# Differential attention on one Trainium2 core: the difference of the two probability maps is made by two matrix products with diagonals of the inverse sums, in place of scaling on VectorE and transposes

## The chip, the cores and the metric

One core of one Trainium2 chip runs the whole program. The time is the device time of one execution in microseconds, and the median of several executions is compared. TensorE (PE in the profile) does the matrix products, VectorE (DVE), ScalarE (ACT) and GpSimd (POOL) the elementwise work; the queues of SyncE (SP) and of ScalarE issue the DMAs.

## The reference

The program is a chain of three transformer blocks over 512 positions of width 1024. Only the attention of the second block is touched. It has 4 heads, each with two maps m = 0, 1 of 64 query and key channels and a common value of 128 channels:

```
logits = einsum('bqhmd,bkhmd->bhmqk', q_blk, k) * scale + bias   # bias by distance, per head
logits = where(causal, logits, -inf)
p = softmax(logits, axis=-1)
attn = p[:, :, 0] - lam_full * p[:, :, 1]
o = einsum('bhqk,bkhe->bqhe', attn, v)
o = rms_norm(o, subln_g, eps=1e-5) * (1.0 - lambda_init)
```

`lam_full` is one number, worked out once from four small vectors. Beside the attention stands a short gated convolution over the other 512 channels, and both go together through one output projection.

## The kernel before, in words

The program is a list of stages. Each stage has a method per engine (`pe`, `act`, `dve`), which writes that engine's instructions in a fixed order by hand; semaphores tie the engines together, and nothing is scheduled by a planner. SyncE streams the weights of the large projections in panels of 1 MB, two buffers deep; it issues nothing that belongs to the attention itself.

The stage is `DiffAttention` (from line 1274 on). Its work is cut into 16 units, head h = 0..3 by query block b = 0..3; unit (h, b) has 128 queries and `nk` = 128(b+1) keys, so one to four key blocks of 128, 40 key blocks over the 16 units. All data are float32. Per unit:

- TensorE makes the logits of each map (lines 1418 and 1419): a product of q and k over 64 rows of the array, and onto it a product of a flipped identity with the bias table, `nk` columns each.
- VectorE takes the maximum of each row (1337) and negates it (1339); ScalarE takes the exponential with that bias and sums each row (1307), which leaves the unnormalised maps in `d_p[:, 0]` and `d_p[:, 1]`, three units deep.
- VectorE takes the reciprocals of both sums (1344), scales map 0 by its own (1346), multiplies the other reciprocal by minus lambda (1347), and adds map 1 times that onto map 0 (1349). Then `probs_ready` is signalled.
- TensorE transposes the difference, one 128x128 block after another, into PSUM bank 5 or 6 (1425).
- VectorE copies the transposed row of blocks to SBUF (1353).
- TensorE multiplies the values with it (1434), accumulated over the key blocks in bank 4 or 7.

The engines run skewed. In its step n TensorE makes the logits of unit n, the transposes of unit n-2 and the products with the values of unit n-3. VectorE in its step n takes the maxima of unit n, the normalisation of unit n-1 and the copy of unit n-2. At the end of a head ScalarE takes the result out and squares it (1295, 1296), TensorE makes its mean squares with products of two columns (1399), VectorE keeps them in `R` (1392, at the top of its steps 8 and 12 for heads 0 and 1), and only then may TensorE transpose the values of the head after the next into the same bank (1411), ahead of that head's first logits.

After the last unit follow the convolution on VectorE and ScalarE (1355 to 1370), 16 diagonals of the inverse roots (1377), their spreading by products with ones (1446), the normalisation (1382) and the split of the result into two parts (1384, 1387). Then the output projection begins (301 to 303). The two products of lines 1425 and 1434 read blocks of 128 columns; `d_w`, which the change adds, lies in the first 768 words of `d_diag`, whose 2048 words are written only after the last unit.

Of the kernel before, what the change touches and what calls it, by code (L numbers as in the profile page):

```python
# [23 lines left out]
ALU = mybir.AluOpType  # L24
# [357 lines left out]
class Stage:  # L382
# [13 lines left out]
    def dve(self, K, P):  # L396
        pass
# [876 lines left out]
class DiffAttention(Stage):  # L1274
# [52 lines left out]
    def dve(self, K, P):  # L1327
        e = P.e
        for n in range(self.N + 2):
            if n >= 8 and n % 4 == 0:  # L1330
                self.keep_mean(K, P, n // 4 - 2)
            if n < self.N:
                h, b = self.UNITS[n]
                nk, st = 128 * (b + 1), K.d_st[:, n % 3]
                for m in range(2):
                    P.e.wait_ge(P.sem("logits_done"), P.due("logits_done"))
                    e.reduce_max(st[:, m, 0:1], K.PS[:, 2 * (n % 2) + m, 0:nk], AX.X).then_inc(P.sem("dve_order"), P.adds("dve_order"))
                    P.e.wait_ge(P.sem("dve_order"), P.due("dve_order", 0))
                    e.tensor_scalar(st[:, m, 1:2], st[:, m, 0:1], -1.0, None, ALU.mult).then_inc(P.sem("max_negated"), P.adds("max_negated"))
            if 1 <= n <= self.N:  # L1340
                nk, st = 128 * (self.UNITS[n - 1][1] + 1), K.d_st[:, (n - 1) % 3]
                p0, p1 = (K.d_p[:, m, (n - 1) % 3, 0:nk] for m in range(2))
                P.e.wait_ge(P.sem("exp_done"), P.due("exp_done", 2))
                e.reciprocal(st[:, :, 3:4], st[:, :, 2:3]).then_inc(P.sem("dve_order"), P.adds("dve_order"))
                P.e.wait_ge(P.sem("dve_order"), P.due("dve_order", 0))
                e.tensor_scalar(p0, p0, st[:, 0, 3:4], None, ALU.mult)
                e.tensor_scalar(st[:, 1, 3:4], st[:, 1, 3:4], K.lamt[:, 5:6], None, ALU.mult).then_inc(P.sem("dve_order"), P.adds("dve_order"))
                P.e.wait_ge(P.sem("dve_order"), P.due("dve_order", 0))
                e.scalar_tensor_tensor(p0, p1, st[:, 1, 3:4], p0, ALU.mult, ALU.add).then_inc(P.sem("probs_ready"), P.adds("probs_ready"))
            if n >= 2:  # L1350
                nk = 128 * (self.UNITS[n - 2][1] + 1)
                P.e.wait_ge(P.sem("probs_transposed"), P.due("probs_transposed"))
                e.tensor_copy(K.d_pT[:, n % 2, 0:nk], K.PS[:, 5 + n % 2, 0:nk]).then_inc(P.sem("probsT_ready"), P.adds("probsT_ready"))

        e.tensor_tensor(K.in2[:, 16:20, :], K.in2[:, 16:20, :], K.in2[:, 20:24, :], ALU.mult).then_inc(P.sem("conv_z"), P.adds("conv_z"))
        self.keep_mean(K, P, 3)
        r = K.R[:, 0:16]
        P.e.wait_ge(P.sem("mean_kept"), P.due("mean_kept", 0))

        e.tensor_scalar(r, r, 1e-5, None, ALU.add).then_inc(P.sem("dve_order"), P.adds("dve_order"))  # L1360
        P.e.wait_ge(P.sem("dve_order"), P.due("dve_order", 0))
        e.reciprocal(r, r).then_inc(P.sem("o_inverse"), P.adds("o_inverse"))
        for i in range(4):
            z, y = K.in2[:, 16 + i, :], K.in2[:, 20 + i, :]
            P.e.wait_ge(P.sem("conv_seeded"), P.due("conv_seeded"))
            e.scalar_tensor_tensor(y[:, 1:S], z[:, 0:S - 1], K.p["conv2_w1"][:, i:i + 1], y[:, 1:S], ALU.mult, ALU.add).then_inc(P.sem("dve_order"), P.adds("dve_order"))
            P.e.wait_ge(P.sem("dve_order"), P.due("dve_order", 0))
            e.scalar_tensor_tensor(y[:, 2:S], z[:, 0:S - 2], K.p["conv2_w0"][:, i:i + 1], y[:, 2:S], ALU.mult, ALU.add).then_inc(P.sem("dve_order"), P.adds("dve_order"))
        P.e.wait_ge(P.sem("dve_order"), P.due("dve_order", 0))
        e.tensor_tensor(K.in2[:, 16:20, :], K.in2[:, 20:24, :], K.in2[:, 12:16, :], ALU.mult).then_inc(P.sem("conv_gated"), P.adds("conv_gated"))  # L1370
        P.e.wait_ge(P.sem("o_root"), P.due("o_root"))

        e.tensor_scalar(r, r, 0.8, None, ALU.mult).then_inc(P.sem("dve_order"), P.adds("dve_order"))
        P.e.wait_ge(P.sem("dve_order"), P.due("dve_order", 0))
        for h in range(4):
            for j in range(4):
                last = e.tensor_scalar(K.d_diag[:, h, 128 * j:128 * j + 128], K.ident[:, :], K.R[:, 4 * h + j:4 * h + j + 1], None, ALU.mult)
            last.then_inc(P.sem("o_diagonals"), P.adds("o_diagonals"))
        for h in range(4):
            P.e.wait_ge(P.sem("o_spread"), P.due("o_spread"))  # L1380
            o = K.in2[:, h, :]
            e.scalar_tensor_tensor(o, o, K.p["subln_g"][:, 0:1], K.PS[:, h, :], ALU.mult, ALU.mult).then_inc(P.sem("o_normed"), P.adds("o_normed"))
        P.e.wait_ge(P.sem("conv_hi"), P.due("conv_hi"))
        e.tensor_tensor(K.XL[:, 4:8, 0:S], K.in2[:, 16:20, :], K.XH[:, 4:8, 0:S].bitcast(F32), ALU.subtract)
        for h in range(4):
            P.e.wait_ge(P.sem("o_hi"), P.due("o_hi"))
            e.tensor_tensor(K.XL[:, h, 0:S], K.in2[:, h, :], K.XH[:, h, 0:S].bitcast(F32), ALU.subtract)
        P.count("att_out_done", 4)
# [5 lines left out]
    def pe(self, K, P):  # L1394
# [7 lines left out]
        for n in range(self.N + 3):  # L1402
            if n < self.N:
                h, b = self.UNITS[n]
                nk = 128 * (b + 1)
                if b == 0:
# [3 lines left out]
                    for j in range(4):  # L1410
                        last = P.e.transpose(K.PS[:, (4, 7)[h % 2], 128 * j:128 * j + 128], K.in2[:, h + 8, 128 * j:128 * j + 128], K.ident[:, :])
# [8 lines left out]
            if 2 <= n < self.N + 2:  # L1420
                m = n - 2
                P.e.wait_ge(P.sem("probs_ready"), P.due("probs_ready"))
                for kb in range(self.UNITS[m][1] + 1):
                    c = slice(128 * kb, 128 * kb + 128)
                    last = P.e.transpose(K.PS[:, 5 + m % 2, c], K.d_p[:, 0, m % 3, c], K.ident[:, :])
                last.then_inc(P.sem("probs_transposed"), P.adds("probs_transposed"))
            if n >= 3:
                h, b = self.UNITS[n - 3]
# [3 lines left out]
                for kb in range(b + 1):  # L1432
                    c = slice(128 * kb, 128 * kb + 128)
                    last = P.e.matmul(K.PS[:, (4, 7)[h % 2], 128 * b:128 * b + 128], K.d_vT[:, h % 2, c],
                                      K.d_pT[:, (n - 3) % 2, c], start=(kb == 0), stop=(kb == b))
# [6 lines left out]
        for h in range(4):  # L1442
            P.e.wait_ge(P.sem("o_diagonals"), P.due("o_diagonals"))
            for j in range(4):
                c = slice(128 * j, 128 * j + 128)
                last = P.e.matmul(K.PS[:, h, c], K.ones_row[:, 0:128], K.d_diag[:, h, c], start=True, stop=True)
# [1068 lines left out]
def program(nc, args, out):  # L2515
    n_panels = args["weights"].shape[0]
    with ExitStack() as ctx:
        K, M = Places(), Mem(nc)
# [34 lines left out]
        def v(name, shape, words, base=None, dt=F32):  # L2553

            assert words + int(np.prod(shape[1:])) <= (room if base is None else 24 * S), (name, room)
            return nc.alloc_sbuf_tensor_at(name, shape, dt, offset=(scr if base is None else base) + 4 * words)
# [26 lines left out]
        K.d_q, K.d_k = (nc.alloc_sbuf_tensor_at(n, [128, 2, 2, S], F32, offset=xa + 4 * 2048 * j) for j, n in enumerate(("d_q", "d_k")))  # L2583
        K.d_p = nc.alloc_sbuf_tensor_at("d_p", [128, 2, 3, S], F32, offset=xb)
        K.d_vT, K.d_pT, K.d_diag = v("d_vT", [128, 2, S], 0), v("d_pT", [128, 2, S], 1024), v("d_diag", [128, 4, S], 2048)
        K.bias, K.d_st, K.lam = v("bias", [128, 4, 512], 5120), v("d_st", [128, 3, 2, 4], 4096), v("lam", [128, 256], 7184)
        K.lamt, K.bias_t, K.onehot = v("lamt", [128, 8], 7440), v("bias_t", [33, 4], 7448), v("onehot", [33, BIAS_W], 7456)
        K.d_sq = v("d_sq", [128, S], 9128)
# [260 lines left out]
```

## Time and profile before

| what | value |
| --- | --- |
| median of 3 runs | 4536.89 us (4536.65 to 4537.7) |
| the profiled execution, its own time | 4535.49 us |
| its span | 4533.7 us |
| mean granted TensorE clock | 0.908 |
| TensorE busy | 3973.9 us, 88% |
| VectorE busy | 2244.2 us, 50% |
| ScalarE busy | 1281.1 us, 28% |
| DiffAttention, first logits to start of the output projection | 1707.8 to 1820.3 us |

The span is the time from the first to the last instruction of the profiled execution, 1.8 us less than its own time; that time is 1.4 us under the median. The clock is given as a share of full speed: 0.50 is 1.2 GHz and 1.00 is 2.4 GHz. A float32 product appears as two MATMULs with a LDWEIGHTS each; a transpose as one of each. Start times of the timeline are in us from the start of the span, and where several instructions are merged the duration is that of all of them, with the last one's latency.

### The profile page before, as it was taken

Reading aid. Unit: us, or ns where it says so; the run is one execution under the profiler, and the core shown is the slowest. Engines: PE = TensorE matmul, PEld = TensorE weight load, DVE = VectorE, ACT = ScalarE, POOL = GpSimd, SP = SyncE. Lnnn points to the kernel's source line nnn. Section 1 sums busy time; section 2 is a strip of 40 time slices with the busy share of each in tenths; the row PEclk is TensorE's granted clock in tenths of the full one; section 3 lists DMA queues with packets and bytes.
Section 4 is the critical chain, followed back from the end, with each engine's and each line's share of the span. In section 5 each row is a group of like instructions: output and inputs, shape, how many; then the busy total and the mean of one; then the engine's idle time right before and its main releaser. Section 6 shows DMA issues by size and latency. Waiting matters only on the chain. (4 is left out here: it accounts for less than half of the span.)

```text
span 4533.7 us, 54286 instructions
## 1 busy us (share of the span) xinstructions
PE 3973.9 (88%) x20865; PEld 3148.3 (69%) x20865; DVE 2244.2 (50%) x3393; ACT 1281.1 (28%) x1779; POOL 0.2 (0%) x4
## 2 busy tenths in 40 slices
PE   7789999978999898799989899782799956998998
PEld 6567887767788774688766688571577734676886
DVE  3475565344646535543443634437566645425344
ACT  2353333221433313222231322223211122223222
POOL 0000000000000000000000000000000000000000
PEclk9999999976999997899997999895899967899998
DMA  3102222210222220122220222220000000022221
GB/s 124 56 0 77 99 93 93 93 37 0 89 97 93 84 95 10 56 93 93 93 80 28 74 93 93 71 73 0 5 0 0 0 13 25 10 83 75 101 95 65
DMA packets 43352, 278.45 MB, mean 61 GB/s; under 512 B 5921, under 2 KB 6817, under 8 KB 10599
## 3 DMA queue, kind: packets, MB, share of 16 engines
q1 hardware_dynamic: 36576, 266.35, 16.7%
q10 hardware_dynamic: 6662, 10.53, 0.7%
q8 instruction: 78, 1.28, 0.1%
q14 instruction: 36, 0.29, 0.0%
HBM read 274.76 MB, written 2.11 MB: 61 GB/s over the span
## 5 line engine op out<-in xcount | busy, mean ns | idle before, releaser
L213 PE MATMUL PS<-XH,WH 128*128 128x512 f32 (+1 forms) x2704 | 1042.7, 386 | 27.3 <-DVEq L95 23.5
L214 PE MATMUL PS<-XL,WH 128*128 128x512 f32 (+1 forms) x2704 | 1044.1, 386 | 0.0
L215 PE MATMUL PS<-XH,WL 128*128 128x512 f32 (+1 forms) x2704 | 1038.7, 384 | 0.0
L146 DVE TENSOR_TENSOR WL<-W,WH 128x2048 fp32r<-128x2048 f32 x254 | 582.1, 2292 | 885.4 <-ACT WH L136 879.9
L136 ACT ACTIVATE WH<-W 128x2048 fp32r<-128x2048 f32 x254 | 485.5, 1912 | 1225.7 <-PE PS L303 681.1
L213 PEld LDWEIGHTS PS<-XH,WH 128*128 128x128 f32 x2704 | 510.6, 189 | 145.2 <-issue 20.2
L214 PEld LDWEIGHTS PS<-XL,WH 128*128 128x128 f32 x2704 | 510.0, 189 | 108.2 <-issue 2.2
L215 PEld LDWEIGHTS PS<-XH,WL 128*128 128x128 f32 x2704 | 511.1, 189 | 103.9
L301 PE MATMUL PS<-HH,WH 128*128 128x512 f32 (+1 forms) x1024 | 402.2, 393 | 10.5 <-DVEq L95 9.3
L484 DVE TENSOR_TENSOR PS<-PS,R 128x512 f32<-128x512 f32 x248 | 171.3, 697 | 467.3 <-PE PS L215 466.8
L302 PE MATMUL PS<-HL,WH 128*128 128x512 f32 (+1 forms) x1024 | 400.3, 391 | 0.0
L303 PE MATMUL PS<-HH,WL 128*128 128x512 f32 (+1 forms) x1024 | 400.0, 391 | 0.0
L301 PEld LDWEIGHTS PS<-HH,WH 128*128 128x128 f32 x1024 | 193.2, 189 | 56.0 <-DVEq L95 10.2
L303 PEld LDWEIGHTS PS<-HH,WL 128*128 128x128 f32 x1024 | 193.2, 189 | 40.5
L302 PEld LDWEIGHTS PS<-HL,WH 128*128 128x128 f32 x1024 | 193.4, 189 | 39.6
L301 PE MATMUL PS<-XH,WH 128*128 128x512 f32 x320 | 130.0, 406 | 26.6 <-DVEq L95 26.6
L736 ACT ACTIVATE CV<-PS,params 128x512 f32<-128x512 f32 x88 | 67.9, 778 | 245.0 <-DVE PS L484 245.0
L302 PE MATMUL PS<-XL,WH 128*128 128x512 f32 x320 | 128.4, 401 | 0.0
L303 PE MATMUL PS<-XH,WL 128*128 128x512 f32 x320 | 128.2, 401 | 0.0
L187 PE MATMUL PS<-XH,WH 128*128 128x512 f32 x144 | 62.2, 432 | 74.4 <-DVE XL L448 74.4
L301 PEld LDWEIGHTS PS<-XH,WH 128*128 128x128 f32 x320 | 62.0, 194 | 42.0 <-DVEq L95 28.1
L187 PEld LDWEIGHTS PS<-XH,WH 128*128 128x128 f32 x144 | 30.0, 208 | 83.9 <-issue 77.0
(446 smaller groups left out, 5220.3 us busy)
## 6 DMA issues: line engine op xcount, KB each, us to landing
W<-in_weights SPq DMA_DIRECT2D x254, 1024.0 KB, 4.8
X<-in_x ACTq DMA_DIRECT2D x1, 2048.0 KB
out<-X ACTq DMA_DIRECT2D x1, 2048.0 KB, 7.1
consts<-in_consts ACTq DMA_DIRECT2D x1, 1026.0 KB
bias<-bias_spread ACTq DMA_DIRECT2D x4, 256.0 KB
w_gd<-in_w_gd ACTq DMA_DIRECT2D x1, 640.0 KB
rope<-in_c_rope ACTq DMA_DIRECT2D x1, 528.0 KB
ws<-in_ws ACTq DMA_DIRECT2D x1, 512.0 KB
```

The lines of the kernel that those rows point to most:

```text
L136: P.e.activation(K.WH[:, s, :], K.W[:, s, :], ACT.Copy).then_inc(P.sem("hi_ready"), P.adds("hi_ready"))
L146: P.e.tensor_tensor(K.WL[:, s, :], K.W[:, s, :], K.WH[:, s, :].bitcast(F32), ALU.subtract).then_inc(P.sem("weights_split"), P.adds("weight ...
L187: P.e.matmul(out, wh[:, k, c], xh[:, k, 0:S], start=(k == 0), stop=False)
L213: P.e.matmul(out, wh[:, k, c], xh[:, k, r], start=(k == 0), stop=False)
L214: P.e.matmul(out, wh[:, k, c], xl[:, k, r], start=False, stop=False)
L215: last = P.e.matmul(out, wl[:, k, c], xh[:, k, r], start=False, stop=(k == KT - 1))
L301: P.e.matmul(out, K.WH[:, s, c], h, start=(first and kk == 0), stop=False)
L302: P.e.matmul(out, K.WH[:, s, c], l, start=False, stop=False)
L303: last = P.e.matmul(out, K.WL[:, s, c], h, start=False, stop=(last_panel and kk == 1))
L484: P.e.tensor_tensor(ps, ps, K.RB[:, :], ALU.mult).then_inc(P.sem("tile_scaled"), P.adds("tile_scaled"))
L736: P.e.activation(K.CV[:, s, t, :], ps[t], ACT.Identity, bias=b[:, c], scale=w[2][:, c]).then_inc(P.sem("conv_seeded"), P.adds("conv_seeded"))
```

## The change

Per unit VectorE no longer touches the maps. From the two reciprocals it makes two diagonal matrices of 128x128: the identity times the inverse sums of map 0, and the identity times the inverse sums of map 1 times minus lambda. TensorE then makes each transposed block of the difference as two float32 products that accumulate in PSUM: block of map 0 against the first diagonal, block of map 1 against the second. The wait on `dve_order` between the old instructions 1347 and 1349 goes with them. Nothing else is moved; no DMA and no ScalarE instruction is touched.

```diff
             if 1 <= n <= self.N:
                 nk, st = 128 * (self.UNITS[n - 1][1] + 1), K.d_st[:, (n - 1) % 3]
-                p0, p1 = (K.d_p[:, m, (n - 1) % 3, 0:nk] for m in range(2))
                 P.e.wait_ge(P.sem("exp_done"), P.due("exp_done", 2))
                 e.reciprocal(st[:, :, 3:4], st[:, :, 2:3]).then_inc(P.sem("dve_order"), P.adds("dve_order"))
                 P.e.wait_ge(P.sem("dve_order"), P.due("dve_order", 0))
-                e.tensor_scalar(p0, p0, st[:, 0, 3:4], None, ALU.mult)
-                e.tensor_scalar(st[:, 1, 3:4], st[:, 1, 3:4], K.lamt[:, 5:6], None, ALU.mult).then_inc(P.sem("dve_order"), P.adds("dve_order"))
-                P.e.wait_ge(P.sem("dve_order"), P.due("dve_order", 0))
-                e.scalar_tensor_tensor(p0, p1, st[:, 1, 3:4], p0, ALU.mult, ALU.add).then_inc(P.sem("probs_ready"), P.adds("probs_ready"))
+                w = K.d_w[:, (n - 1) % 3]
+                e.tensor_scalar(w[:, 0, :], K.ident[:, :], st[:, 0, 3:4], None, ALU.mult)
+                e.tensor_scalar(w[:, 1, :], K.ident[:, :], st[:, 1, 3:4], K.lamt[:, 5:6], ALU.mult, ALU.mult).then_inc(P.sem("probs_ready"), P.adds("probs_ready"))
...
                 for kb in range(self.UNITS[m][1] + 1):
                     c = slice(128 * kb, 128 * kb + 128)
-                    last = P.e.transpose(K.PS[:, 5 + m % 2, c], K.d_p[:, 0, m % 3, c], K.ident[:, :])
+                    P.e.matmul(K.PS[:, 5 + m % 2, c], K.d_p[:, 0, m % 3, c], K.d_w[:, m % 3, 0, :], start=True, stop=False)
+                    last = P.e.matmul(K.PS[:, 5 + m % 2, c], K.d_p[:, 1, m % 3, c], K.d_w[:, m % 3, 1, :], start=False, stop=True)
                 last.then_inc(P.sem("probs_transposed"), P.adds("probs_transposed"))
...
+        K.d_w = v("d_w", [128, 3, 2, 128], 2048)
```

## Rows read from the trace of the kernel before

**Rows 1.** Busy time by stretch: span, PE, PEld, DVE, ACT, POOL, clock, DMA, GB/s.

```profile
1705.40:1731.40 26.00, 24.73 (x45) 10.65 (x45) 7.82 (x28) 9.66 (x24) 0.00 (x0) 0.50 0.00 0
1731.40:1769.00 37.60, 34.70 (x157) 20.62 (x157) 23.97 (x79) 18.23 (x50) 0.00 (x0) 1.00 0.00 1
1769.00:1786.00 17.00, 17.00 (x45) 10.15 (x44) 7.59 (x25) 3.60 (x13) 0.00 (x0) 0.50 0.00 0
1786.00:1799.20 13.20, 9.99 (x53) 6.38 (x52) 8.16 (x18) 4.66 (x11) 0.00 (x0) 1.00 0.00 1
1799.20:1820.30 21.10, 5.95 (x32) 5.76 (x32) 19.21 (x38) 7.20 (x10) 0.00 (x0) 0.67 0.00 0
```

**Rows 2.** Waits of 1705 to 1821 us: us in total, times, longest.

```profile
DVE d_st L1337 <- PE PS L1419: 47.6, 29, 9.2
...
PE PS L1411 <- DVE R L1392: 2.9, 2, 1.4
```

**Rows 3.** Groups of instructions by form, 1712 to 1830 us: busy us, mean ns.

```profile
L1425 PE MATMUL PS<-consts,d_p 128*128 128x128 f32 x40 | 8.5, 316 | 1.9 <-DVE d_p L1349 1.9
...
L1377 DVE TENSOR_SCALAR d_diag<-consts,R 128x128 f32<-128x128 f32 x16 | 3.2, 278 | 0.0
```

**Rows 4.** Timeline at full clock: start, duration, engine, line, instruction.

```profile
1736.35 0.60 PE L1425 MATMUL PS<-consts,d_p 128*128 128x128 f32 x4
1736.78 0.83 PE L1434 MATMUL PS<-d_pT,d_vT 128*128 128x128 f32 x6
1737.55 0.91 PE L1418 MATMUL PS<-d_k,d_q 64*128 64x384 f32 x2
```

**Rows 5.** Timeline of TensorE at half clock.

```profile
1775.14 1.06 PE L1425 MATMUL PS<-consts,d_p 128*128 128x128 f32 x4
1775.99 1.49 PE L1434 MATMUL PS<-d_pT,d_vT 128*128 128x128 f32 x6
```

**Rows 6.** Timeline of TensorE around the rise of the clock.

```profile
1729.64 0.64 PE L1425 MATMUL PS<-consts,d_p 128*128 128x128 f32 x2
...
1731.49 0.49 PE L1418 MATMUL PS<-d_k,d_q 64*128 64x128 f32 x2
```

**Rows 7.** Timeline where the third head begins.

```profile
1747.03 0.16 DVE L1344 RECIPROCAL d_st<-d_st 128x2 f32<-128x2 f32 x1
...
1748.67 0.15 DVE L1392 COPY R<-PS 128x4 f32<-128x4 f32 x1
...
1748.88 0.66 PE L1411 MATMUL PS<-consts,in 128*128 128x128 f32 x4 [1.45 <-DVE R L1392]
1749.47 0.37 PE L1418 MATMUL PS<-d_k,d_q 64*128 64x128 f32 x1
```

**Rows 8.** Timeline of TensorE where the fourth head begins.

```profile
1763.05 1.13 PE L1419 MATMUL PS<-bias,consts 128*128 128x512 f32 x2
...
1764.46 0.95 PE L1399 MATMUL PS<-consts,d_sq 128*128 128x2 f32 x8
1766.86 0.66 PE L1411 MATMUL PS<-consts,in 128*128 128x128 f32 x4 [1.45 <-DVE R L1392]
1767.44 0.48 PE L1418 MATMUL PS<-d_k,d_q 64*128 64x128 f32 x2
```

**Rows 9.** Timeline of the last three units.

```profile
1788.98 1.13 PE L1419 MATMUL PS<-bias,consts 128*128 128x512 f32 x2
...
1790.94 0.16 DVE L1344 RECIPROCAL d_st<-d_st 128x2 f32<-128x2 f32 x1
...
1791.71 0.62 DVE L1349 SCALAR_TENSOR_TENSOR d_p<-d_p,d_st 128x384 f32<-128x384 f32 x1
...
1792.38 0.55 PE L1425 MATMUL PS<-consts,d_p 128*128 128x128 f32 x3 [1.05 <-DVE d_p L1349]
...
1794.29 0.66 PE L1425 MATMUL PS<-consts,d_p 128*128 128x128 f32 x4 [0.86 <-DVE d_p L1349]
...
1794.99 0.69 DVE L1353 COPY d_pT<-PS 128x512 f32<-128x512 f32 x1 [0.28 <-PE PS L1425]
```

## The prediction

> **What bounds the kernel now.** The table by engine says little by itself: TensorE is busy 88% of the span and VectorE 50%, over dozens of stages. What counts is the stage that is touched, 1705 to 1820 us, so the first view is busy time by stretch [rows 1]. Until 1786 TensorE is busy 24.7 of 26.0, 34.7 of 37.6 and 17.0 of 17.0 us, VectorE at most two thirds. Only behind 1799 is it the other way round: VectorE 19.2 of 21.1 us, TensorE 6.0. The second view, the waits, names who waits [rows 2]: VectorE waits for the logits for 47.6 us in 29 pieces, TensorE waits for VectorE in a few places only. In its main part the stage is thus bound by TensorE, and the change takes work from VectorE and gives it to TensorE. The two exceptions matter. TensorE idles twice for 1.45 us until VectorE has kept the means [rows 7, 8], and twice at the end until VectorE has normalised, 1.05 and 0.86 us [rows 9].
>
> The same stretches show a second thing: the granted clock is 0.50 (1.2 GHz) from 1705.4 to 1731.4 and again from 1769 to 1786, and 1.00 (2.4 GHz) between [rows 1]. In the first of them TensorE was hardly idle and stayed at 1.2 GHz all the same.
>
> **What is added to TensorE.** There are 40 key blocks, one transpose each, one MATMUL per transpose [rows 3]. A float32 product of the same size is two MATMULs, so two products are four where one stood. Four transposes at full clock begin 0.43 us before the next group, 0.107 us each; six MATMULs of the products with the values take 0.77 us to the start of the next, 0.128 us each with the change to other operands included [rows 4]. At half clock four transposes take 0.85 us, 0.212 us each [rows 5]. I take 0.107, since the new MATMULs follow each other in fours to sixteens as those do, and the change to other operands was there before, once per unit. The upper bound is 0.128; below 0.107 nothing goes, as no row has a MATMUL of 128 columns that follows quicker. Three more per block are 0.32 us at full clock and 0.64 us at half.
>
> The Trainium skill, page "Perfetto Trace Analysis", section Transposes, speaks against this change: logical transposes should be made with the transpose, not with an ordinary product. It gives no price. By that rule alone the result would be slower; by the rows it is slower by what follows, and the rest of the sum decides.
>
> Step by step, with the places of the old trace:
>
> - *Units 0 and 1* (3 blocks), at half clock: 9 MATMULs by 0.212, 1.9 us. But the transposes of unit 1 stood at 1729.6 and the clock rose before 1731.5 [rows 6]. If it rises at the same moment, some 9 MATMULs that ran just before it now run behind it, at 0.107 instead of 0.212, which gives 0.95 us back. Net 0.95 us.
> - *Units 2 to 12* (28 blocks: 7, 10, 10 and 1), at full clock: 28 by 0.32, 9.0 us, all in TensorE's stream with nothing to cover it. At 0.128 per MATMUL it would be 2.4 us more.
> - *Units 13, 14 and 15*: below, 0.6 us.
>
> **What is taken from VectorE.** For a unit of 384 keys the four old instructions last from 1790.94 to 1792.33 (start of the reciprocal to the end of line 1349), 1.39 us [rows 9]. The new ones: 0.19 us for the reciprocal and its wait, then two of the form of line 1377, 128x128 from the identity, 16 of which took 3.2 us, 0.20 us apart and 0.28 us long [rows 3]. The row has one scalar; the second diagonal has two. I take the same price; the bounds are 0.28 and 0.48 us, as if it were two such instructions. That is 0.67 us, 0.7 us less. Where TensorE is the one waited for, this is worth nothing: it lengthens VectorE's idle time. It is worth something at four places.
>
> - *The two starts of a head.* From the reciprocal to the keeping of the means VectorE took 1.64 us, and the values' transposes waited [rows 7]. VectorE is now ready 0.7 us sooner and TensorE arrives 0.64 us later, two blocks of a unit 5 or 9 (which are among the 28). The idle time of 1.45 us shrinks to some 0.4 us, the time for the last means to land, be kept and be seen. Gain 1.05 us each, 2.1 us together. Bounds: 0.64 us each (covered anyway) and the whole 1.45.
> - *The end.* After the last logits TensorE had 2 blocks of unit 13, two products, the means of head 2, and then waited until 1792.38 and 1794.29 for VectorE; the last transposes had landed by 1794.99 [rows 9]. Now unit 14 is ready at about 1791.6 on the same scale and TensorE gets to it at 1791.95 (0.64 us of unit 13 fall into the old wait). Its 12 MATMULs take 1.28 us, the products with the values 0.45, and the 16 of unit 15 1.71 us: 1795.4, landed by 1795.6. That is 0.6 us later than before. Here VectorE's gain pays for nine blocks all but 0.6 us. What is late next is TensorE itself. The following chain (result out, squares, mean, then VectorE's convolution) moves by the same 0.6 us.
>
> Sum without the clock: 0.95 + 9.0 - 2.1 + 0.6 = 8.45 us slower.
>
> **The clock.** It fell at 1769, right behind the start of the fourth head: eight MATMULs of two columns (0.95 us), then 1.45 us of idle time, then short products [rows 8]. The same sequence at the third head did not bring it down [rows 1, 7], so the case is a close one. In the new kernel 0.64 us of dense products stand ahead of it and the idle time is 1.05 us shorter, which should keep the clock up here. What the low stretch cost can be read by comparing two heads: from the first logits to the last of the head, 1749.47 to 1763.05, 13.6 us at full clock, and 1767.44 to 1788.98, 21.5 us for the fourth [rows 7 to 9]. So its loss is worth 8.0 us. I take it as the likelier case. The sum becomes 8.45 - 8.0 = 0.45 us slower. The sum is made on the profiled execution (4535.49 us, 1.4 us under the median); I add it to the median: 4536.9 + 0.45 = 4537.4 us.
>
> **Rivals.**
>
> *The low stretch stays.* Place: 1769 to 1786. The point from which it decides is whether the clock still falls behind the fourth head's start. Then 8.0 us are not gained, and the 8 blocks of units 10 to 12 cost 3 by 0.105 us more each, 2.5 us: 8.45 + 2.5 = 11 us slower, 4547.9 us. For it: it fell before, and the first stretch shows that a busy TensorE can stay at 1.2 GHz for over 20 us. Against it: the shorter pause. Chance 0.24.
>
> *The clock rises sooner in the first stretch.* The new products of units 0 and 1 are dense work in the middle of it. If it rose behind those of unit 0, at about 1722, 9.4 us of work would run at twice the pace: 4.7 us less than in my forecast, 4532.7 us. For it speaks that the rise came just as transposes and products of 128 columns stood side by side [rows 6]; against it, that one block of unit 0 is a small part of that work. Chance 0.08. The Trainium skill, page "TensorE: Matmul & The Clock Gate", section Part 4: PE-mode transpose, says that a transpose does not count as activity for the clock; by that rule the products in its place would favour this rival. The rows have transposes and products together just ahead of the rise and do not decide it [rows 6].
>
> *VectorE was the bound after all*, and the difference is made sooner everywhere. Then its 0.3 to 0.9 us a unit, some 10 us, would come off and TensorE's 9 us would be hidden: 4527 us. Against it stands that TensorE has no wait for the maps but in the last two units. Chance 0.02.
>
> *Something later moves.* The rest of the program runs unchanged but at another moment, and the places where the clock falls and rises can shift with it. The mean clock of 0.908 says that such stretches are common. I give my forecast 4 us on either side for this; with a larger effect, of either sign, 0.06.
>
> **How the numbers follow.** The forecast has 0.60. About 9 us (0.2%) is what a measurement of this kernel can tell from no change. Forecast and early rise lie inside. The rival of 11 us lies beyond it by 2 us, with 4 us of play, so some 0.17 of its 0.24 is slower by more; 0.04 comes from the bounds of my own sum (2.4 us for dearer MATMULs, 0.8 us for smaller gains at the heads) together with play, and 0.03 from later shifts. Slower 0.24, faster 0.04, same 0.72. The range runs from 4531 (early rise and some play) to 4549 (the rival). The likeliest case alone is 4533 to 4542.
>
> **What would show it.** Line 1425 in two lines with 160 MATMULs in place of 40, of the same mean duration; VectorE about 10 us less busy; waits of line 1411 for VectorE under 1 us in all; none of the last units for VectorE's maps; the clock at 1.00 from 1731 to beyond 1790. The forecast is wrong if the stretch of 0.50 behind 1769 is still there (then the time is near 4548), if line 1425's MATMULs follow each other slower than 0.107 us, or if the stage is unchanged in length but the stages behind it are not.

## The result, and the profile after

The changed kernel takes 4544.33 us in the median of 20 runs (4541.65 to 4546.14), the kernel before 4537.09 us in 20 runs beside it (4534.75 to 4540.35): a ratio of 1.0015, interval 1.0008 to 1.0022. That is 7.2 us slower, within the 0.2% that was called no change, and within the range; the forecast had 0.45 us. But the forecast's own case was 4533 to 4542 us, and the result lies beyond it. The stated range reached to 4549 us only for the rival in which the low stretch stays, and that did not happen: that the result fell inside is luck. The profiled execution took 4544.81 us, its span is 4543.0 us.

Everything of this program starts 2.5 us later in this profile than in the one before; that part belongs to the single execution (a second profile of the changed kernel has 1.1 us) and is taken off where places are compared. Busy time by stretch of the changed kernel, the first four cut as [rows 1] and moved by 2.5 us (span, PE, PEld, DVE, ACT, POOL, clock, DMA, GB/s):

```profile
1707.90:1733.90 26.00, 24.73 (x46) 11.22 (x47) 6.62 (x24) 9.10 (x23) 0.00 (x0) 0.50 0.00 0
1733.90:1771.50 37.60, 37.34 (x195) 24.55 (x194) 18.13 (x63) 16.69 (x45) 0.00 (x0) 1.00 0.01 1
1771.50:1788.50 17.00, 16.75 (x99) 12.35 (x99) 8.45 (x31) 5.30 (x17) 0.00 (x0) 1.00 0.00 0
1788.50:1801.70 13.20, 11.91 (x75) 8.78 (x75) 7.14 (x17) 4.17 (x11) 0.00 (x0) 1.00 0.01 1
1801.70:1823.30 21.60, 6.35 (x39) 6.07 (x38) 19.26 (x38) 8.02 (x11) 0.00 (x0) 0.67 0.00 0
```

The third line is the one to read: where the clock stood at 0.50 for 17 us, it is 1.00, and TensorE issues 99 MATMULs there instead of 45. The first low stretch is unchanged, and from there to 1788 TensorE is busy but for two pauses of 0.26 us. Where the fourth head begins, the timeline of TensorE answers to [rows 8]:

```profile
1773.49 0.95 PE L1397 MATMUL PS<-consts,d_sq 128*128 128x2 f32 x8
1774.70 0.66 PE L1409 MATMUL PS<-consts,in 128*128 128x128 f32 x4 [0.26 <-DVE R L1390]
1775.29 0.48 PE L1416 MATMUL PS<-d_k,d_q 64*128 64x128 f32 x2
```

The pause is 0.26 us instead of 1.45. The new instructions by form, 1712 to 1830 us (busy us, mean ns), answer to [rows 3]:

```profile
L1423 PE MATMUL PS<-d_w,d_p 128*128 128x128 f32 x80 | 16.2, 286 | 0.0
L1424 PE MATMUL PS<-d_w,d_p 128*128 128x128 f32 x80 | 16.0, 282 | 0.0
...
L1347 DVE TENSOR_SCALAR d_w<-consts,d_st,lamt 128x128 f32<-128x128 f32 x16 | 5.5, 341 | 0.0
L1346 DVE TENSOR_SCALAR d_w<-consts,d_st 128x128 f32<-128x128 f32 x16 | 4.6, 286 | 0.6
```

There are 160 MATMULs for 40, and none waits for VectorE. And a piece of the timeline at full clock, which answers to [rows 4]:

```profile
1776.86 0.39 PE L1423 MATMUL PS<-d_w,d_p 128*128 128x128 f32 x2
1777.08 0.39 PE L1424 MATMUL PS<-d_w,d_p 128*128 128x128 f32 x2
1777.31 0.39 PE L1423 MATMUL PS<-d_w,d_p 128*128 128x128 f32 x2
```

A product of two MATMULs every 0.223 us: 0.112 us each, for which 0.107 had been taken.

To find where 7 us came from, I measured the stage in every profile, from its first logits to the first MATMUL of the output projection: 112.6 us in the kernel before (both profiles of it), 113.1 and 112.9 us in the changed kernel. The stage costs 0.4 us more, as forecast. From there to the last MATMUL of the program it is 2699.8 and 2699.9 us before, 2706.2 and 2706.0 us after. The time is lost behind the stage, in code that the change doesn't touch. The experiments had two questions: is the stage's 0.4 us the sum that was claimed, and what is late behind it?

### The profile page after: what moved, and what is told of

It reads as the page before. It is cut to its first block and busy times, and to the rows that moved or that the text cites. A ratio compares the mean times of both kernels' runs of the same rounds, so it can differ in the third digit from the quotient of the medians.

```text
span 4543.0 us, 54510 instructions
## 1 busy us (share of the span) xinstructions
PE 3985.2 (88%) x20985; PEld 3158.7 (70%) x20985; DVE 2237.5 (49%) x3377; ACT 1281.5 (28%) x1779; POOL 0.2 (0%) x4
## 5 line engine op out<-in xcount | busy, mean ns | idle before, releaser
L301 PE MATMUL PS<-HH,WH 128*128 128x512 f32 (+1 forms) x1024 | 401.7, 392 | 10.5 <-DVEq L95 9.3
L301 PEld LDWEIGHTS PS<-HH,WH 128*128 128x128 f32 x1024 | 193.1, 189 | 56.0 <-DVEq L95 10.2
```

The lines of the kernel that those rows point to most:

```text
L301: P.e.matmul(out, K.WH[:, s, c], h, start=(first and kk == 0), stop=False)
```

## The experiments

Medians of 9 to 11 runs each; the kernel before had 4538.0, 4537.6 and 4536.2 us in the three groups of four.

**Two profiles more.** The kernel before, unchanged:

> The kernel before, once more, to see how far two profiles of one kernel differ. My theory (the attention stage itself costs only 0.5 us more after the change, because the low-clock stretch behind the fourth head's start is gone, and the other 7 us come from stretches of low clock outside the stage) expects 4537 us, the stretch of 0.50 at 17 us length behind the fourth head, and the stage at 112.5 us from its first transposes less 2 to the output projection, within 0.5 us. The rival (the 7 us are a difference between executions, not between kernels) expects that this profile's shift against the first profile of before is as large as that of the changed kernel, 3 to 9 us in places outside the stage.

4537.68 us. Against the first profile no MATMUL in the whole program is moved by more than 0.4 us. The changed kernel, unchanged:

> The changed kernel once more. My theory expects 4544 us, no stretch of 0.50 between 1734 and 1799 us, and the additional low stretches of the first profile (behind 2266, 2403, 2512 and 3648 us) at the same places. The rival (they are chance) expects other places and a total that wanders by several us.

4544.09 us. The clock stays up from 1732 to 1800 us, and the additional low stretches lie at the same places as in its first profile, two of them 3.4 us shorter. So the 6 us behind the stage belong to the kernel. The comparison of profiles is finer than the medians: executions of the kernel before range from 4535 to 4544 us, and its two profiles are of 4535.5 and 4535.3 us, so a difference between profiles may overstate that between medians.

**VectorE's half alone.** In the changed kernel, leaving out the scaling and the second map:

```diff
-                    P.e.matmul(..., K.d_p[:, 0, m % 3, c], K.d_w[:, m % 3, 0, :], start=True, stop=False)
-                    last = P.e.matmul(..., K.d_p[:, 1, m % 3, c], K.d_w[:, m % 3, 1, :], start=False, stop=True)
+                    last = P.e.transpose(..., K.d_p[:, 0, m % 3, c], K.ident[:, :])
```

> VectorE's half of the change alone: two diagonals per unit are made, but TensorE transposes map 0 as before, unscaled; leaves out the scaling and the second map. If TensorE is the bound and VectorE's gain counts only at the two heads' starts and at the end: 0.6 us less at each head's start and 1.3 us less at the end, 2.5 us in all, so the stage takes 110 us; 8 us less again if the low stretch behind the fourth head's start goes with a pause of 0.85 us in place of 1.45. The rival that VectorE is the bound expects 10 us less in the stage with the clock as it was.

4529.21 us, and the stage took 102.1 us, 10.5 us less. The trace parts the sum: from its first to its last logits the fourth head takes 14.1 us in place of 22.1, the pauses at the third and fourth head's start are 0.65 us shorter each, and the end is 1.2 us shorter: 8.0 and 2.5. The low stretch behind the fourth head's start is gone. TensorE's pause there, in this run:

```profile
1767.26 0.66 PE L1409 MATMUL PS<-consts,in 128*128 128x128 f32 x4 [0.79 <-DVE R L1390]
```

Its 10.5 us equal the rival's 10 us, so the total alone would not have told them apart; the clock does. At 1.00 from 1733 to 1791 us:

```profile
1733.00:1791.00 58.00, 53.85 (x253) 32.63 (x251) 33.13 (x111) 27.36 (x73) 0.00 (x0) 1.00 0.00 1
```

**TensorE's half alone.** In the kernel before, with `d_w` added and one block of it set to zero:

```diff
-                    last = P.e.transpose(..., K.d_p[:, 0, m % 3, c], K.ident[:, :])
+                    P.e.matmul(..., K.d_p[:, 0, m % 3, c], K.ident[:, :], start=True, stop=False)
+                    last = P.e.matmul(..., K.d_p[:, 1, m % 3, c], K.d_w[:, 0, 0, :], start=False, stop=True)
```

> TensorE's half alone: VectorE scales and subtracts as before, TensorE makes each block with two products, one with the identity and one with a block of zeros. 28 blocks in mid-stream 9.0 us, units 0 and 1 1 us, 0.64 us covered at each of the two heads' starts, about 1.3 us at the end: 10 us more with the clock as before; 2 us more if the low stretch behind the fourth head's start goes, since the pause there shrinks to 0.8 us. The rival that the added products are hidden expects no change in the stage.

4543.66 us (4538.3 to 4548.6; the profiled execution is the slowest of them), the stage 116.2 us, 3.6 us more. The pause was 0.78 us; the clock fell all the same, but came back after 3.4 us:

```profile
1776.00 0.65 PE L1412 MATMUL PS<-consts,in 128*128 128x128 f32 x4 [0.78 <-DVE R L1393]
```

```profile
1734.00:1778.40 44.40, 42.85 (x231) 28.97 (x230) 25.28 (x84) 19.07 (x51) 0.00 (x0) 1.00 0.00 1
1778.40:1781.80 3.40, 3.40 (x17) 3.17 (x16) 2.40 (x7) 0.62 (x4) 0.00 (x0) 0.50 0.00 0
1781.80:1805.00 23.20, 21.54 (x123) 15.08 (x122) 13.45 (x35) 6.20 (x17) 0.00 (x0) 1.00 0.00 1
```

3.4 us at half speed cost 1.6 us (the fourth head takes 18.4 us from its first to its last logits, and 16.8 in the changed kernel); without them the stage would be 2.0 us longer, as expected. The products are not hidden.

**The means kept early.** If the pause is what brings the clock down, the kernel before can have the gain without the change:

```diff
-            if n >= 8 and n % 4 == 0:
-                self.keep_mean(K, P, n // 4 - 2)
+            if n == 16:
+                self.keep_mean(K, P, 2)
...
+            if n in (7, 11):
+                self.keep_mean(K, P, n // 4 - 1)
             if 1 <= n <= self.N:
```

> The kernel before with the means of heads 0 and 1 kept ahead of the normalisation of the unit that stands in between, so that TensorE's pause at the third and fourth head's start shrinks from 1.45 to some 0.4 us, with nothing added to TensorE. Theory (the shorter pause keeps the clock up): low stretch of 17 us behind the fourth head's start gone, stage 8 + 2 = 10 us shorter, 102.5 us, total 4527 to 4531. Rival (it was the added dense products of 128 columns that kept the clock up): the low stretch stays, stage 2 us shorter, total 4535.

4526.23 us, ratio 0.9977 (0.9967 to 0.9987): faster than both kernels, with not one instruction more or less. The stage takes 102.3 us. Its stretches:

```profile
1708.70:1732.40 23.70, 23.70 (x41) 9.93 (x41) 7.86 (x29) 7.36 (x21) 0.00 (x0) 0.50 0.00 0
1732.40:1790.50 58.10, 53.67 (x252) 32.62 (x251) 40.31 (x124) 27.01 (x73) 0.00 (x0) 1.00 0.00 1
1790.50:1811.00 20.50, 6.03 (x33) 5.84 (x33) 18.57 (x35) 6.49 (x8) 0.00 (x0) 0.58 0.00 0
```

and its fourth head's start:

```profile
1765.40 0.66 PE L1413 MATMUL PS<-consts,in 128*128 128x128 f32 x4 [0.26 <-DVE R L1394]
```

So the 17 us at half clock go without the change, with VectorE's scaling and the transposes as they were. The fourth head takes 14.1 us in place of 22.1, as in VectorE's half alone. What the run does not part is the length of the pause and the moment at which it comes: the pause at the third head's start shrank too, and everything behind it stands 1.2 us sooner. This version also gives the change its true price: with the clock up in both and the pause 0.26 us in both, the changed kernel's stage is 113.0 - 102.3 = 10.7 us longer. By the prediction's terms it would be 0.95 + 9.0 + 0.6 = 10.55 us, the pauses left out.

**The pause put back into the changed kernel**, first with four copies of 256 columns ahead of `keep_mean` at n = 12:

```diff
+            if n == 12:
+                for j, k in ((2, 0), (3, 0), (1, 256)):
+                    e.tensor_copy(K.d_diag[:, j, k:k + 256], K.ones_row[:, 0:256])
+                e.tensor_copy(K.d_diag[:, 2, 256:512], K.ones_row[:, 0:256])
```

> The changed kernel with four copies of 128x256 on VectorE ahead of keeping the means at the fourth head's start alone, so that TensorE's pause there grows from 0.26 to about 1.3 us while the added products stay. Theory (the pause decides): the low stretch behind the fourth head's start is back, stage 1 + 8 to 10 us longer, total about 4553. Rival (the added products keep the clock up): only the pause itself, 1.1 us more, total 4545.

4544.66 us, and the stage only 0.2 us longer, since its end came out 0.4 us shorter. The pause had grown to 0.93 us, not to the 1.3 meant, and the clock stayed up:

```profile
1774.58 0.66 PE L1413 MATMUL PS<-consts,in 128*128 128x128 f32 x4 [0.93 <-DVE R L1394]
1733.10:1804.80 71.70, 66.75 (x372) 46.33 (x371) 36.83 (x120) 29.36 (x74) 0.00 (x0) 1.00 0.00 1
```

So once more, with five such copies and two of 512 columns:

> The changed kernel with VectorE's copies ahead of the means of the fourth head's start made longer, so that TensorE's pause there grows to about 1.9 us; with 0.93 us the clock had stayed up. Theory (the pause decides): the clock falls behind the fourth head's start, stage 1.6 + 8 to 10 us longer than 113 us. Rival (the added dense products keep the clock up, or the pause counts only where it falls at an unlucky moment): stage about 1.3 us longer, 114.3 us, total 4545.

```profile
1770.60 0.95 PE L1402 MATMUL PS<-consts,d_sq 128*128 128x2 f32 x8
1773.35 0.66 PE L1414 MATMUL PS<-consts,in 128*128 128x128 f32 x4 [1.80 <-DVE R L1395]
```

```profile
1731.00:1775.30 44.30, 42.24 (x226) 28.36 (x225) 22.16 (x80) 18.79 (x49) 0.00 (x0) 1.00 0.00 1
1775.30:1778.70 3.40, 3.40 (x17) 3.40 (x18) 1.35 (x7) 0.92 (x4) 0.00 (x0) 0.51 0.00 0
1778.70:1802.00 23.30, 22.01 (x128) 15.57 (x127) 11.90 (x32) 6.47 (x17) 0.00 (x0) 1.00 0.00 1
```

4547.06 us; the stage 116.2 us, 3.1 more: 1.5 us of pause and 1.6 us for 3.4 us at half clock. Both theories were half right. With the longer pause the clock falls. But what stays low for 17 us in the kernel before is over after 3.4 us where the products of 128 columns stand, and both runs with these products show that.

All pauses at the fourth head's start together: with 0.26 us the clock stayed up in all five profiles, with 1.45 or 1.80 us it fell in all six. Between them the length does not decide: with 0.93 us here and 0.79 us in VectorE's half it stayed up, with 0.78 us in TensorE's half it fell. And the pause of 1.45 us at the third head's start never brought it down. So what stands around the pause, or the moment at which it comes, counts too; no run parts these.

**What is late behind the stage.** I compared the start of every MATMUL behind the stage with the first profile of the kernel before. The time is lost at few places, the same in many kernels. Growth in us in each stretch, places by the trace of before (0 stands for less than 0.3); `DVE` is how many instructions more or less than in the kernel before VectorE executed in all, semaphore instructions included:

```
kernel                        DVE  2250-2300 2370-2540 2880-2960 3200-3260 3260-3600 3640-3665 4060-4200
changed                       -16    1.6       1.2       0.3       0         1.4       1.6       0
changed, again                -16    1.2       1.1       0         0         1.4       1.2       0
VectorE's half                -16    1.0       0.8       0         0         1.3       1.5       0
changed, pause of 0.93        -12    1.2       1.1       0         0         1.3       1.6       2.7
changed, pause of 1.80         -9    1.6       1.2       0.3       2.5       1.3       0         0
TensorE's half                  0    1.2       1.2       0        -0.4       0         2.6       3.0
changed, old program length     0    1.3       1.2       0         0         0         0         2.6
before, longer multiply         0    0         0         0         0         0         0         0
early means                     0    0         0         0         0         0         0         0
before + one copy              +1    0         0         1.9       2.9       0         1.5       0
before + one idle instruction  +1    0         0         1.9       2.9       0         1.3       2.6
early means + one copy         +1    0         0         1.9       3.0       0         1.4       0
```

The rows of TensorE's half and of the idle instruction are the slowest execution of their kernel, and several kernels with the products also gain or lose up to 0.6 us before 1900 us (VectorE's half 1.5 us less). The last column follows nothing that I can name. In TensorE's half the added memset takes the place of a semaphore instruction, so that VectorE's program is as long as before, and not one instruction longer, as the expectation below has it.

The stretch 3260 to 3600 is a loop of the third block. VectorE's first instruction of a pass, and what it idled before, in the kernel before and, in the second fence, in the changed one (a line's view: us, times):

```profile
L2007 DVE TENSOR_TENSOR c_r<-PS,block_mask x33: 691/692/693, 3220.9 to 3639.1; 128x512 f32<-128x512 f32 x33
...
  DVE rz L2033: 6.6, 16
```

```profile
L2006 DVE TENSOR_TENSOR c_r<-PS,block_mask x33: 691/691/692, 3226.6 to 3646.4; 128x512 f32<-128x512 f32 x33
...
  DVE rz L2032: 8.2, 16
```

0.1 us more in each of 16 passes, at the branch back. There is nothing in the loop that the change touches; what moved is where the loop lies in VectorE's program, which is shorter by one instruction and one wait a unit. Hence this run, in the changed kernel:

```diff
+                e.memset(K.d_diag[:, 3, 0:1], 0.0).then_inc(P.sem("dve_order"), P.adds("dve_order"))
+                P.e.wait_ge(P.sem("dve_order"), P.due("dve_order", 0))
                 w = K.d_w[:, (n - 1) % 3]
```

> The changed kernel with VectorE's program brought back to its old length: per unit one more tiny instruction and one more wait, 32 in all. In the traces so far the branch back at the end of the third block's recurrence loop is followed by VectorE's next instruction after 0.29 us in the changed kernel and in the run of VectorE's part, and after 0.19 us in the kernel before and in the run of TensorE's part, whose VectorE program is one instruction longer than before. Theory: this depends on where the loop lies in VectorE's program. Expects pairs of steps of 26.12 us (12.87 + 13.25) there again instead of 26.23, 1.7 us less over the loop; the attention stage 0.2 to 0.5 us longer; total 4542.5 to 4543. Rival: the loop is slower because the stage before it ended at another moment; expects 26.23 still.

4540.48 us (4538.2 to 4543.7), 3.6 us less than the changed kernel's second median, with 16 instructions and 16 waits *more*; beside it the kernel before took 4537.55 us. The stage is as long as before this edit, 113.1 us, and the loop is back at its old pace:

```profile
L2008 DVE TENSOR_TENSOR c_r<-PS,block_mask x33: 690/692/692, 3224.7 to 3643.0; 128x512 f32<-128x512 f32 x33
...
  DVE rz L2034: 6.6, 16
```

The loss at 3640 us is gone too. The theory held for the loop: in the table the five profiles with a shorter program lose there, and no other does. The place at 3640 us does not follow the length: the changed kernel with the long pause, 9 instructions short, loses nothing there, and TensorE's half, with the old length, loses 2.6 us.

For the rest I then held the small delay of the stage responsible. In the kernel before, behind the last unit:

```diff
         self.keep_mean(K, P, 3)
+        e.tensor_copy(K.d_p[:, 1, 1, 0:512], K.d_p[:, 0, 1, 0:512])
```

> The kernel before with one copy of 128x512 put into VectorE's chain behind the last unit, some 0.4 us. Theory (stretches of low clock behind the stage grow by a small delay alone): the stage 0.4 us longer, and one or more of the low stretches behind 2264, 2400, 2510 and 3642 us longer by 3.4 us each at 1.7 us of time each, total 4540 to 4544. Rival (the delay is not the cause; the low stretches grow with another thing of the change, such as the length of a program): total 4538, the stretches as they were.

4543.25 us, as this theory had it, though the stage is only 0.15 us longer (112.7 us). Two runs to part delay and instruction, one memset of one column at n = 3, where VectorE waits anyway, and one multiplication on 400 columns instead of 16:

> The kernel before with one tiny instruction more in VectorE's program, put where VectorE waits for the logits of unit 3, so that nothing is late. The run with one copy more behind the last unit ended the stage only 0.15 us later, yet was some 5 us slower in all, with longer low stretches behind 2898 and 3217 and at 3646 us. Theory (a small shift in time behind the stage tips the later low stretches): no shift here, total 4537 to 4538, stretches as before. Rival (one instruction more moves the later loops in the program, and that does it): 4542 to 4544.

> The kernel before with no instruction more: the multiplication by 0.8 behind the convolution takes 400 columns instead of 16 (the added ones are not used), which makes the stage 0.2 us longer. Theory (a small shift in time tips the later low stretches): total 4541 to 4544 with one or more stretches longer by 3.4 us. Rival (the program's length does it): 4538.

4544.06 us (ratio 1.0016, 1.0007 to 1.0025) and 4536.73 us (0.9999). My theory fell. One idle instruction costs 7.8 us against the kernel before in the same group, with a stage of 112.5 us. The delay did not come about either: the longer multiplication left the stage at 112.6 us, so that run tells nothing of a delay, only that an edit that adds no instruction leaves every later place where it was. A delay of 0.4 us and more, as the changed kernel has it, stays untested by itself. Where the loss begins can be seen at 2917 us. The last lines before the place, first the kernel before, then the one with the idle instruction, 2.4 us later throughout:

```profile
2915.32 1.89 DVE L703 TENSOR_TENSOR X<-X,Y 128x512 f32<-128x512 f32 x3
2916.03 1.85 ACT L620 ACTIVATE Y<-X 128x528 f32<-128x528 f32 x3 [0.62 <-DVE X L703]
2917.41 1.95 DVE L658 TENSOR_TENSOR Y<-Y 128x528 f32<-128x528 f32 x3 [0.20 <-ACT Y L620]
```

```profile
2917.73 1.89 DVE L703 TENSOR_TENSOR X<-X,Y 128x512 f32<-128x512 f32 x3
2918.45 1.85 ACT L620 ACTIVATE Y<-X 128x528 f32<-128x528 f32 x3 [0.62 <-DVE X L703]
2920.20 1.94 DVE L658 TENSOR_TENSOR Y<-Y 128x528 f32<-128x528 f32 x3 [0.58 <-ACT Y L620]
```

VectorE starts 0.38 us later, with the same work ahead of it and its input as ready as before. That costs little by itself. But TensorE begins its next work later by it, and its clock then stays down for 3.4 us more, which costs another 1.5 us. The 0.58 us stand there in all three kernels with one VectorE instruction more, and 0.20 or 0.21 us in the eleven other profiles, with -16 to 0 instructions. The same moment of both kernels, 44.4 us behind the fall of the clock:

```profile
2943.20:2946.60 3.40, 3.40 (x17) 2.92 (x16) 0.00 (x0) 0.00 (x0) 0.00 (x0) 1.00 0.00 0
```

```profile
2945.60:2949.00 3.40, 3.40 (x10) 2.58 (x9) 0.00 (x0) 0.00 (x0) 0.00 (x0) 0.50 0.00 0
```

**The quick version under the same test.** The early means with the copy behind the last unit:

> The version with the means kept early (4526 us) with the copy that was put behind the last unit in the earlier run. Asks how much of its gain of 11 us hangs on where the later low stretches fall. Theory: the stage keeps its 10 us, the rest wanders by up to 6 us: 4526 to 4533. Rival (the gain itself rests on the later stretches): 4536.

4533.87 us, ratio 0.9994 (0.9985 to 1.0003), no longer clear of the kernel before: 2.4 us of the 11.3 are left, each against its own group, and the time is 0.9 us above what the theory allowed. The stage kept its 102.4 us; the loss is at the three places of every kernel with one VectorE instruction more. So the 10 us in the stage are real, and one VectorE instruction took most of them back from the total.

## Why the prediction was right, and where not

*Inside the stage* the sum holds term by term. It can be read from the first and last logits of each head in the first profile of each kernel; from the third head's first logits to the fourth's, for example, it was 17.97 us and is 20.15, for 10 blocks and a pause that is 1.19 us shorter:

| term | forecast | measured |
| --- | --- | --- |
| units 0 and 1 | 0.95 | 1.03 |
| the 28 blocks | 9.0 | 9.42 |
| the two heads' starts | -2.1 | -2.38 |
| the end | 0.6 | 0.40 |
| the low stretch | -8.0 | -7.95 |
| sum | 0.45 | 0.52 |

*TensorE's added MATMULs*: they follow each other in 0.112 us, not 0.107. That is one of the signs that the forecast named for being wrong; it is worth the 0.4 us of the second line. That nothing covers them was shown by TensorE's half alone.

*VectorE's gain* counts only at the heads' starts and at the end: VectorE's half alone gave the 2.5 us expected for these, and no more. The pauses shrank to 0.26 us (0.4 forecast). The second diagonal takes 0.34 us, not 0.28; VectorE's total fell by 6.7 us, from 2244.2 to 2237.5, and not by the 10 that I named as a sign, without any effect on the time. Some 4.5 us of waits of VectorE for the new products (line 1351 for line 1424) are new and harmless.

*The clock* was the step on which the forecast stood, and it came out: the low stretch behind the fourth head's start is gone, its worth was put at 8.0 us, and the two versions that lose it without TensorE's part show 10.5 us (2.5 of them the waits) and 10.3 us (2.3). That it goes with the early means alone shows that the added products are not needed for it. That the length of the pause is the reason is not shown: lengths of 0.78 to 0.93 us gave both outcomes. Where the clock does fall, the runs with the products have it back after 3.4 us.

*The early rise* in the first stretch did not come: it ends at 1733.9 us, 2.5 us later like everything else. The Trainium skill's rule that transposes don't count for the clock (page "TensorE: Matmul & The Clock Gate", section Part 4: PE-mode transpose) had no effect that could be seen in this stretch. Behind the fourth head's start the clock came back after 3.4 us with the products and after 17 with the transposes. That would fit the rule, but there are also four MATMULs for each one, and no run parts the two.

*The low stretch stays* and *VectorE was the bound* were wrong in the changed kernel, by its third stretch and by the waits.

What failed is the step "something later moves". It was priced as a symmetric play of 4 us that comes from a shift in time, with the forecast's centre untouched, and with a chance of 0.06 for more. Measured are 6.4 and 6.1 us behind the stage in the two profiles of the changed kernel, all to one side. "The stage unchanged in length but the stages behind it not" was the last of the forecast's own signs of being wrong, and it is what came about. Of the first profile's 6.4 us, 1.4 are shown to hang on VectorE's program length: the loop whose branch back takes 0.1 us longer. I had counted instructions only by what they cost in the stage. The rest is pieces of 1 to 1.6 us, most of them with 3.4 us more of low clock, and what brings them is open. The one at 3640 us does not follow the length. Those at 2250 to 2300 and 2370 to 2540 us, 2.8 us together, stay when the length is restored. They appear in every kernel whose stage is 0.4 us or more longer than before, and in VectorE's half (10.5 us shorter); they are missing where the stage's length is within 0.15 us of before, and in the two kernels with the early means (10.2 and 10.3 us shorter). So the shift in time that the prediction named may well be what brings these; no run moved the end of the stage by itself.

## What to carry to other kernels

Before work is shifted between engines, look at the short pauses of TensorE just ahead of a fall of its clock: here 8 us at the fourth head went with one of 1.45 us, though the same pause at the third head cost nothing but itself. Moving one small copy of VectorE ahead of five other instructions won 10.3 us in the stage, as much as leaving out the scaling and the second map. A change of a few instructions moves everything behind it in that engine's program; at 0.1 to 0.2% an experiment needs a control with one idle instruction, and an A/B on totals alone can't price an edit. The two halves of a change, each alone, and the time of the stage itself told more here than the total, which was 7 us slower for an edit that costs 0.4 us where it stands.

## What the runs showed of the hardware

One memset of a single column, put where its engine was idle, made a 4536 us program 7.8 us slower. VectorE's first instruction behind the branch of a loop came 0.1 us later in 16 of 16 passes, in all five profiles of kernels with 9 to 16 VectorE instructions less and in none of the nine others. Its first instruction at another place came 0.38 us later in the three kernels with one instruction more and in none of the others. Nothing at either place had been edited. Why the length of the program does this was not asked by any run.

TensorE's clock amplified this: a start 0.4 us later went with 3.4 us more at 1.2 GHz. The clock also stayed at 1.2 GHz for 23.7 us in which TensorE was busy all the time (1708.7 to 1732.4 us, early means), with products over 64 and 128 rows in turn. The low stretch to which this belongs is 37.5 or 37.6 us long in every profile, whatever the edit.
